# A relative bias table built and spread in DRAM during the first MLP, and parameter rows sent through GpSimd's queue, in a fused two-block transformer kernel on one core

## The reference

```python
def first_block(x, p, ...):
    h = rmsnorm(x, norm_mix_g)
    u_rwkv, u_attn, u_gate = split(h @ w_in)
    merged = g_a * (rwkv7(u_rwkv) @ w_proj_a) + g_b * (diff_attention(u_attn) @ w_proj_b)
    x = x + merged @ w_out
    x = x + square(relu(rmsnorm(x) @ w_ff1)) @ w_ff2          # "first MLP"
    return x + (p @ w_ple) * sigmoid(rmsnorm(x) @ w_ple_gate)

def second_block(x, p, ..., rel_bias):
    h = rmsnorm(x, ln1) @ w_in                                 # GLA, attention, gates
    for g, (win, dil) in enumerate(((128, 1), (512, 4), (2048, 16))):
        # bias[h, q, k] = rel_bias[bucket(max(q + 128 - k, 0) * dil), 4 * g + h]
        outs, lses = dilated_attention(q, k, v, bias_of_group(rel_bias, g), dil, win // dil)
    ...                                                        # same tail as the first block
```

## Time and profile before

| what | us |
|---|---|
| median of 3 runs (lowest, highest) | 2008.54 (2007.86, 2010.1) |
| the profiled execution's own time | 2005.89 |
| its span in the trace | 2004.1 |
| PE busy | 1929.7 (96%) |
| DVE busy | 1017.7 (51%) |
| ACT busy | 738.4 (37%) |
| POOL busy | 87.3 (4%) |

### The profile page before, as it was taken

One profiled execution on the slowest core, in us unless ns is written; L12 is line 12 of the kernel. 1 busy time (PEld: TensorE's weight loads), 2 busy tenths in 40 slices (PEclk: granted clock), 3 DMA queues, 4 the chain that ended last, 5 costly groups with the idle time before them and its releaser, 6 DMA issues.

```text
span 2004.1 us, 23341 instructions
## 1 busy us (share of the span) xinstructions
PE 1929.7 (96%) x9550; PEld 1580.5 (79%) x9550; DVE 1017.7 (51%) x1717; ACT 738.4 (37%) x1184; POOL 87.3 (4%) x135
## 2 busy tenths in 40 slices
PE   6999999999999999999469999999999999999997
PEld 5787778778888888887358888899888888888886
DVE  4768574447644444567343433623345744443544
ACT  6444454333432323244243422433223432323233
POOL 1000111102000000000000000000000000000000
PEclk9999999999999999999789999999999999999999
DMA  5233310217333232324842222222354333232321
GB/s 198 83 86 101 91 39 28 74 64 263 94 96 105 86 103 85 105 84 85 69 130 85 64 85 84 85 84 90 108 171 139 102 107 98 91 105 84 104 86 43
DMA packets 174179, 194.58 MB, mean 97 GB/s; under 512 B 13350, under 2 KB 151761, under 8 KB 174072
## 3 DMA queue, kind: packets, MB, share of 16 engines
q1 hardware_dynamic: 169720, 181.70, 30.5%
q0 software_dynamic: 2768, 9.08, 1.3%
q10 hardware_dynamic: 1584, 2.30, 0.3%
HBM read 177.57 MB, written 15.49 MB: 96 GB/s over the span
## 4 chain that ended last, share of the span: by engine, by line
PE 92%; SPq 4%; DMA 1%; ACT 1%; DVE 1%; issue 0%; POOLq 0%; ACTq 0%
PE bank L130 90%; SPq L118 4%; PE bank L133 2%; DMA raw<-in_w_in_dram 1%; ACT L140 0%; ACT wh L140 0%; ACT GP L140 0%; ACT xt L140 0%; ACT LD L140 0%; DVE wl L154 0%; DVE T L154 0%; ACT AP L141 0%; DVE KI L154 0%; DVE LS L154 0%; ACT T L140 0%
## 5 line engine op out<-in xcount | busy, mean ns | idle before, releaser
L140 ACT ACTIVATE wh<-raw 128x1024 fp32r<-128x1024 f32 (+1 forms) x299 | 315.9, 1057 | 769.0 <-PE bank L130 711.1
L130 PE MATMUL bank<-XH,wh 128*128 128x512 f32 (+1 forms) x1272 | 508.0, 399 | 7.8 <-ACT wh L140 7.8
L154 DVE TENSOR_TENSOR wl<-raw,wh 128x1024 fp32r<-128x1024 f32 x298 | 366.3, 1229 | 280.4 <-ACT wh L140 279.6
L130 PE MATMUL bank<-XL,wh 128*128 128x512 f32 (+1 forms) x1272 | 497.8, 391 | 2.2 <-DVE XL L162 2.2
L130 PE MATMUL bank<-XH,wl 128*128 128x512 f32 x1264 | 324.4, 394 | 0.0
L130 PEld LDWEIGHTS bank<-XH,wh 128*128 128x128 f32 (+1 forms) x1272 | 239.3, 188 | 64.9 <-ACT wh L140 6.0
L130 PEld LDWEIGHTS bank<-XL,wh 128*128 128x128 f32 (+1 forms) x1272 | 239.6, 188 | 51.3 <-DVE XL L162 3.3
L130 PEld LDWEIGHTS bank<-XH,wl 128*128 128x128 f32 x1264 | 233.6, 188 | 52.0 <-issue 4.3
L130 PE MATMUL bank<-mid,wh 128*128 128x512 f32 x1024 | 243.8, 389 | 0.0
L130 PEld LDWEIGHTS bank<-mid,wh 128*128 128x128 f32 x1024 | 192.2, 188 | 39.9
L154 DVE TENSOR_TENSOR T<-bank,RST 128x512 f32<-128x512 f32 x122 | 84.1, 689 | 234.1 <-PE bank L130 233.9
(11 more groups left out here) (410 smaller groups left out, 2307.0 us busy)
## 6 DMA issues: line engine op xcount, KB each, us to landing
raw<-in_w_in_dram SPq DMA_DIRECT2D x58, 1024.0 KB, 5.2
raw<-in_w_ff_dram SPq DMA_DIRECT2D x32, 1024.0 KB, 5.2
raw<-in_w_mlp_dram SPq DMA_DIRECT2D x32, 1024.0 KB, 5.3
raw<-in_w_out_dram SPq DMA_DIRECT2D x8, 1024.0 KB, 5.6
scr_x<-XT POOLq DMA_DIRECT2D x16, 256.0 KB, 12.3
XT<-scr_x SPq DMA_DIRECT2D x8, 512.0 KB, 7.4
raw<-in_w_ple_gate_dram SPq DMA_DIRECT2D x4, 1024.0 KB, 5.1
raw<-in_w_o_gla_dram SPq DMA_DIRECT2D x4, 1024.0 KB, 5.5
```

Source lines behind the costliest of these rows:

```text
L130: return self.put(ns, lambda e: e.matmul(out, lhsT, rhs, start=start, stop=stop, skip_group_check=True))
L140: return self.put(ns, lambda e: e.activation(out, in_, func, bias=bias, scale=scale), func)
L154: return self.put(self.ns(out), lambda e: e.tensor_tensor(out, a, b, op))
```

## The change

It has five edits.

1. **The relative bias moves to the first MLP.** `pl_rel_bias` and `dv_rel_bias` wait for the weights of the gated input (`pw`, `pwh`) in place of `plep 7`, and the two products stand behind the transposed p of the first block (`ppl 0 1`). The tiles move to pages that are free then. The product p·w_ple (`pe_ple_product`) now waits for `browc 1`, since it takes the same banks.
2. **The row is spread from DRAM, by POOL.** In place of SP's 12 DMAs POOL writes brow once to a small array in DRAM (scr_row, 12 x 896), waits for it, and issues three DMAs from scr_row to scr_b, DRAM to DRAM.
3. **The first weight chunk is 256 columns** in one buffer, in two loads of 128 columns with a semaphore each; the second chunk, now a full one, follows at once in the other buffer. Every later chunk lies in the other buffer than before.
4. **The 16 p_rows loads go through POOL**, at the head of its "spill" lane; SP's other parameter loads wait for the first half chunk, and the first ALB load for rst0.
5. **Order.** The fourth Square waits for XH 3, and the "lo" lane is due by the first XH·wl product of its unit (`need_lo`) in place of the unit's first product.

```diff
@@ sp_w
+            if ci == 0:
+                sp.dma_start(raw[:, :, 0:128], src[:, :, 0:128]).then_inc(*self.sig("rawa").up16(("first", 0)))
+                sp.dma_start(raw[:, :, 128:256], src[:, :, 128:256]).then_inc(*self.sig("rawb").up16(("first", 1)))
+            else:
+                sp.dma_start(raw, src).then_inc(*self.sig(f"raw{ci % NRAW}").up16(("chunk", ci)))
@@ ac_hi
-            ac.wait_ge(self.at("chunk", u["chunk"]))
+            ac.wait_ge(self.at("chunk", u["chunk"]) if u["chunk"] else self.at("first", u["i"]))
@@ under
+        if k0 == 0 and j == 0:
+            self.need_lo[u["i"]] = self.mm
@@ pe_ple_product
-        pe.wait_ge(self.at("pbf", n - 4) if n >= 4 else self.at("imp", 0))
+        pe.wait_ge(self.at("pbf", n - 4) if n >= 4 else self.at("browc", 1))
@@ sp_params, split
-    def sp_params(self, s):
-        sp, a = self.sp, self.a
+    def pl_params(self, s):
+        pl, a = self.pl, self.a
         for name, k in PARAMS[1:]:
             ...
-            sp.dma_start(self.p_rows[r0:r0 + k, :], ...)
+            pl.dma_start(self.p_rows[r0:r0 + k, :], ...)
+
+    def sp_params(self, s):
+        sp, a = self.sp, self.a
+        yield
+        sp.wait_ge(self.at("first", 0))
         sp.dma_start(self.LW[0:64, :], a["rwkv_w2"][0])...
@@ ac_begin
-            ac.wait_ge(self.at("xs", j))
+            ac.wait_ge(self.at("xs", j), *([self.at("h", "X0", 3)] if j == 3 else []))
@@ the ALB loads
-            if h:
-                sp.wait_ge(self.at("mx", h - 1, 3, 1))
+            sp.wait_ge(self.at("mx", h - 1, 3, 1) if h else self.at("rst0"))
@@ plan_block1
-        for c in (1536, 1664):
-            plan("rw", w, 0, 8, c, 128, "n", 1)
+        plan("rw", w, 0, 8, 1536, 256, "n", 2)
@@ pl_rel_bias, dv_rel_bias
-        pl.wait_ge(self.at("plep", 7))
+        pl.wait_ge(self.at("pw", 0), self.at("pwh", 0, 1))
...
-        dv.wait_ge(self.at("plep", 7))
+        dv.wait_ge(self.at("pwh", 0, 1), self.at("pw", 0))
@@ pe_rel_bias
-            pe.wait_ge(self.at("relpad"), self.at("rel"), self.at("pbf", 6 + x))
+            pe.wait_ge(self.at("relpad"), self.at("rel"), self.at("ppl", 0, 1), self.at("imp", 0))
@@ the spread
-    def sp_rel_bias(self, s):
-        sp = self.sp
+    def pl_copy_bias(self, s):
+        pl = self.pl
+        yield
+        pl.wait_ge(self.at("browc", 1))
+        pl.dma_start(self.scr_row, self.brow[:, :]).then_inc(*self.sig("brow").up16(("browd",)))
         for g, (c0, n) in enumerate(((0, 384), (384, 256), (640, 256))):
-            for h in range(4):
-                yield
-                sp.wait_ge(self.at("browc", 1))
-                sp.dma_start(self.scr_b[g][h:h + 1], bc(self.brow[4 * g + h:4 * g + h + 1, c0:c0 + n], 1, 128))...
+            yield
+            pl.wait_ge(self.at("browd"))
+            pl.dma_start(self.scr_b[g], bc(self.scr_row[4 * g:4 * g + 4, c0:c0 + n], 1, 128))...
@@ arrange, due()
-                    return max(t, clock["pe"]) + 227 * (self.need[l.unit_of[l.i]] - dense) - (2500 if l.name == "lo" else 5000)
+                    need, lead = (self.need_lo, 2500) if l.name == "lo" else (self.need, 5000)
+                    return max(t, clock["pe"]) + 227 * (need[l.unit_of[l.i]] - dense) - lead
```

More of the change, by code:

```diff
@@ L236, in __init__ @@
         self.tile, self.guard, self.last_use = {}, {}, {}
-        self.chunks, self.units, self.need, self.bank, self.bank_after = [], [], {}, {}, {}
+        self.chunks, self.units, self.need, self.need_lo, self.bank, self.bank_after = [], [], {}, {}, {}, {}
         self.fixed_tiles()
@@ L344, in sp_w @@
                 sp.wait_ge(self.at("lo", self.chunks[ci - NRAW]["last"]))
-            sp.dma_start(self.raw[ci % NRAW][:, 0:nk * ncol].rearrange("p (k n) -> p k n", k=nk),
-                         c["w"][128 * c["k0"]:128 * (c["k0"] + nk), c["c0"]:c["c0"] + ncol].rearrange("(k p) n -> p k n", p=128)
-                         ).then_inc(*self.sig(f"raw{ci % NRAW}").up16(("chunk", ci)))
+            raw = self.raw[ci % NRAW][:, 0:nk * ncol].rearrange("p (k n) -> p k n", k=nk)
+            src = c["w"][128 * c["k0"]:128 * (c["k0"] + nk), c["c0"]:c["c0"] + ncol].rearrange("(k p) n -> p k n", p=128)
+            if ci == 0:
[3 more added lines that the diff above has]
+                sp.dma_start(raw, src).then_inc(*self.sig(f"raw{ci % NRAW}").up16(("chunk", ci)))
     def ac_hi(self, s):
@@ L382, in next_unit @@
         self.unit_i += 1
-        self.need[u["i"]] = self.mm
+        self.need[u["i"]] = self.need_lo[u["i"]] = self.mm
         return u
@@ L612, in sp_params @@
             r0 = self.col[name] - 8
-            sp.dma_start(self.p_rows[r0:r0 + k, :], v.rearrange("(r p) -> r p", p=128)).then_inc(*self.sig("par").up16(("prows",)))
+            pl.dma_start(self.p_rows[r0:r0 + k, :], v.rearrange("(r p) -> r p", p=128)).then_inc(*self.sig("par").up16(("prows",)))
+    def sp_params(self, s):
+        sp, a = self.sp, self.a
+        yield
+        sp.wait_ge(self.at("first", 0))
         sp.dma_start(self.LW[0:64, :], a["rwkv_w2"][0]).then_inc(*self.sig("lw").up16(("lw",)))
@@ L1965, in pe_norms @@
         yield from self.pe_ple(s, 0)
+        yield from self.pe_rel_bias(s)
         yield from self.pe_mean_squares(s, "rst1", self.ACC, self.ps[4], ("ysa", 0, 7), ("ysqd", 0, 0), ("imb", 0))
         yield from self.pe_spread(s, "rst1", self.T[2], self.ps[4], ("ms1",))
-        yield from self.pe_rel_bias(s)
         yield from self.pe_mean_squares(s, "m1", self.ACC, self.ps[4], ("sqp", 7), ("rst1",))
@@ L1982, in dv_norms @@
         yield from self.dv_ple(s, 0)
+        yield from self.dv_rel_bias(s)
         yield
@@ L1986, in dv_norms @@
         yield from self.dv_spread(s, "rst1", self.rs, self.T[2])
-        yield from self.dv_rel_bias(s)
         yield
@@ L2052, in block2_tiles @@
         self.scr_x2 = scratch("scr_x2", (8, 128, 512))
-        self.rel, self.hot, self.brow = m("rel", 41, [33, 12]), m("hot", 42, [33, 896]), m("brow", 44, [12, 896])
+        self.rel, self.hot, self.brow = m("rel", 33, [33, 12], off=1600), m("hot", 32, [33, 896]), m("brow", 34, [12, 896])
+        self.scr_row = scratch("scr_row", (12, 896))
         self.scr_b = [scratch("scr_b0", (4, 128, 384)), scratch("scr_b1", (4, 128, 256)), scratch("scr_b2", (4, 128, 256))]
@@ L2833, in pool_lanes @@
         yield "merge", 500, lambda s: self.chain(self.pl_merge(s), self.pl_blank2(s))
-        yield "spill", 2000, lambda s: self.chain(self.pl_keep(s), self.pl_ple(s, 0, a["p"][0, 0], a["w_ple"][0]), self.pl_rel_bias(s), self.pl_spill2(s), self.pl_load_bias(s),
+        yield "spill", 2000, lambda s: self.chain(self.pl_params(s), self.pl_keep(s), self.pl_ple(s, 0, a["p"][0, 0], a["w_ple"][0]), self.pl_rel_bias(s), self.pl_copy_bias(s), self.pl_spill2(s), self.pl_load_bias(s),
                                                   self.pl_dil(s), self.pl_ple(s, 1, a["p_2"][0, 0], a["w_pp_2"][0]), self.pl_lnf(s))
@@ L2840, in sync_lanes @@
         yield "attn", 0, lambda s: self.chain(self.sp_attn(s), self.sp_block2(s), self.sp_last(s))
-        yield "spill", 1000, lambda s: self.chain(self.sp_spill1(s), self.sp_rel_bias(s), self.sp_merge2(s))
+        yield "spill", 1000, lambda s: self.chain(self.sp_spill1(s), self.sp_merge2(s))
         yield "load", 1000, self.sp_load1
```

2 lines of the change are left out of this document (1 added, 1 removed).

## The result

The changed kernel takes 1956.24 us, the median of 4 runs (1953.57 to 1958.7), against 2008.62 before (4 runs): 0.9738 of it, 95% interval 0.972 to 0.9756, 52.4 us less. Forecast were 48.3 us less and 1960.2; rival A of the prediction stood at 54.0 less and 1954.5. The profiled execution takes 1953.57 us, its span is 1951.8, and TensorE is busy for 99% of it.

A forecast was written before the change was run, and what follows sets the result against it. TensorE was taken as the bound, 96% busy, its idle time mostly a wait on KI behind SP's queue. Middle 45.6 + MLP 0 + begin 2.7 = 48.3 us off 2008.54, giving 1960.2 us; range 1952 to 1971.

The forecast's parts named there:

- rival A: Begin: the ISA instruction is short (up to 1.3 us), begin gives 8.4, sum 54.0, 1954.5 us; chance 0.17.
- The middle, 45.6 us: Near 970 to 1034 us: removing the spread ends TensorE's wait on KI and its slow clock; 45.6 us (43.6 to 46.6).
- A queue, not a bandwidth.: Middle: the weight load was late because it stood behind SP's 59.20 us of issuing 12 spreading DMAs; bytes matter less.
- The new place in the MLP, 0: First MLP: the moved relative bias and spread cost TensorE nothing; 0 us.
- my upper bound of 10: First MLP: most the spread could cost through weight loads landing in 14.3 us each; 10 us.
- The begin, 2.7: Kernel's begin: earlier third unit and smaller waits, 8.4 less 5.7, give 2.7 us (-1.6 to 9.8).
- X: Begin: price of the ISA instruction ahead of POOL's power; taken as 5.7 us, from a span of 0 to 10.07.
- my formula: Begin's gain: third unit's earlier start, 0.66 wait and slow clock; up to 9.8 us less the ISA instruction's price.
- the third unit at about 31 and a wait of 5 us ahead of T_58: Begin, signs of being right: third unit's first product at about 31 us, TensorE waiting some 5 us before T_58's transposes.
- p_rows at nothing: Begin: moving the 16 p_rows loads from SP to POOL was counted as nothing, since nobody reads them before 20 us.
- C: Middle or MLP: another wait replaces the removed one, 12 or 10 us back; 1970 to 1975 us; chance 0.12.
- D: First MLP: the DRAM-to-DRAM copy holds back weight loads, slower than before, about 2012 us; chance 0.03.

The follow-up runs named there:

- E1: Changed kernel with only the relative-bias part (first MLP, spread from DRAM by POOL), begin and order as in the kernel before; 1959.99 us.
- E4: Begin as changed, relative bias at its old place, the same 12 spreading DMAs from SBUF rows issued by POOL instead of SP; 2006.47 us.
- E5: Kernel before, at the old time on SP's queue, spread from DRAM by way of scr_row in three DMAs; 1964.83 us.
- E7: Changed kernel with the old spread, 12 DMAs from SBUF rows on SP's queue, in the first MLP; 2001.63 us.
- E6: E4 with the spread from DRAM by way of scr_row, in three DMAs by POOL at the old time; 1954.61 us.
- E9: E5 with the three DMAs turned so that the 128 copies are the outermost dimension; 1960.93 us.
- E2: Changed kernel with only the begin and order edits, relative bias computed and spread as in the kernel before; 2000.21 us.
- E3: Changed kernel plus one more power on POOL, on constants nobody reads, ahead of all but one parameter load; 1954.73 us.
- E10: Changed kernel with the 16 p_rows loads issued by SP again, without SP's wait for the first half chunk; 1961.38 us.
- E8: The changed kernel again, unedited; 1955.67 us.

## Why the prediction was right, and where it was wrong

The time was near enough (48.3 forecast, 52.4 measured), the middle's term was right in size, and its reason was wrong. The time is nearer to rival A's (54.0 us, 1954.5) than to the forecast, and A's mechanism of the begin is the one that came.

- *The middle, 45.6 us.* Measured 46.0 between the landmarks, 47.5 in E1. Its parts came as worked out: the wait and the slow clock behind it went, and one small wait of 0.9 stands in their place, where I had taken 1.0.
- *"A queue, not a bandwidth."* This failed. E4 took the spread off the queue and the wait stayed, at 48.0. E5 left the queue alone and changed the source, and the wait went. The mistake was in the 14.3 us that I took as the price of a load in the crowd: that load was issued at 998.51, when the spread's last DMA had been issued. What would have told was in the trace: the window of 941 to 959 with 0.87 busy at 29 GB/s, and POOL's eight spills of scr_x, issued from 955.8 to 960.4 in a queue in which nothing of the spread stood. Their time to landing, before and after the change:

```profile
DMA to landing us min/median/max: 15.3/32.5/33.0
```

```profile
DMA to landing us min/median/max: 3.3/3.5/4.0
```

- *The new place in the MLP, 0.* Right, and for a reason that I had not priced: the spread now takes about 15 us, and the longest landing of a weight load beside it is 8.4. With the old source it costs a wait of 42.8 there (E7), four times my upper bound of 10. Edit 1, the move itself, is worth nothing that can be measured (E6). POOL's queue, with the move, is worth some 4 us in the form that the change has, 4 rows outermost (E1's 47.5 for E5's 43.0), and nothing once the copies are outermost (E9's 47.1). The source in edit 2 is the gain.
- *The begin, 2.7.* Measured 5.8 in the trace, 7.2 in E2, 4.9 as what E1 leaves of the whole. The term that was mis-sized is X, taken as 5.7: it is 0.1 to 0.24 (E3 and the trace after), so rival A has the mechanism. The rule of the Trainium skill on the first call of a freshly loaded kernel, "GPSIMD Engine Reference", "Instruction dispatch", doesn't show here: no such 6 us stands ahead of either power. With X = 0 my formula gives 9.8, and two things that it left out take 3.9 back. TensorE came to T_58's place at 22.36, not at 20 to 21 (the formula's 20.3): behind the wait on XL it ran at the lower clock, 1.2 GHz, for seven products (13.28 to 16.40, 0.446 us each), which cost 1.5 us, and it waited 0.82 for XT. (Ahead of T_58 the traces show 16 wh products before and 24 with four wl after, where the section on the change has 12 and 20; the 32 and 20 products behind it, by which I reckoned, are right.) And the wait on LD grew from 0.66 to 1.81, where I had it go. That leaves 9.8 - 2.1 - 1.8 = 5.9. Of my signs for the begin, the third unit at about 31 and a wait of 5 us ahead of T_58, neither came; T_58 was on time, which I had named as A's.
- *p_rows at nothing.* Wrong by the size of the whole begin: 5.7 us (E10), of which the slow clock behind the longer wait is more than half. I asked who reads p_rows and who stands behind them on SP at the third chunk, and not what the DMA engines do meanwhile.
- *Rivals.* C and D did not come; D would have, by 46.0 us, had the source stayed in SBUF (E7). What saved the forecast was an edit whose worth I had not seen.
- The scatter of single runs, 1952.9 to 1958.7 for the same kernel, is as large as the begin. A part of it is the clock's fall at about 280 us with TensorE busy (E8); what brings that about stays open.

## What to carry to other kernels

Read the DMA engines' busy share together with their GB/s: a share near 0.9 at 27 to 30 GB/s was here a transfer that held up all others, in whichever queue they stood, and a load's landing time is to be taken where the crowd begins, not where it ends. Before a transfer is moved to a quieter place, change its form: a broadcast out of one SBUF row took 4 times as long as one through a small array in DRAM (59 us for 15), and on SP's queue that goes faster still with the copies as the outermost dimension. Tiny loads on the queue that also issues the large ones cost DMA engines' time that stands idle, even if nobody reads them early, and a wait of TensorE can cost as much again in the slow clock behind it (E10: 3.5 and 4.2 us).

## What the runs showed of the hardware

- A broadcast of one SBUF row to DRAM ran at 29 to 30 GB/s with the DMA engines 0.83 to 0.87 busy, at two places (before, E7), and a 1 MB load beside such a spread from POOL's queue took 58.5 us (E4) in place of 5.2. A packet of some 1.4 KB held an engine for 0.71 us, from DRAM for 0.067 (before, E5).
- The issue of the 12 DMAs held SP for 59.20 us (before) and POOL for 6.21 (E4).
- The same copy from DRAM with 4 rows outermost kept to a share of 0.24 from SP's queue (E5), had 0.41 from POOL's (the changed kernel), and with 128 outermost was issued from SP in 3.11 us for 11.06 (E9).
- The ISA instruction ahead of POOL's first power took 0.1 us (E3).
- TensorE's granted clock fell to 0.50 for some 7 us while the engine waited for nothing, in some executions of a kernel and not in others (E8; the changed kernel).
